# Finer pieces for the first weights, x and the third unit at the opening of a two-layer hybrid encoder trunk

## The reference

```python
for l in range(DEPTH):                      # DEPTH = 2
    h = rms_norm(x, ffn1_norm[l])
    x = x + 0.5 * swiglu(h, ffn1_w_gate[l], ffn1_w_up[l], ffn1_w_down[l])   # 1024 -> 2816 -> 1024
    h = rms_norm(x, mix_norm[l])
    p = h @ w_in[l]
    ...        # three groups of heads: forgetting attention, HGRN2 recurrence, S5 state space
    x = x + mix @ w_out[l]
    h = rms_norm(x, ffn2_norm[l])
    x = x + 0.5 * swiglu(h, ffn2_w_gate[l], ffn2_w_up[l], ffn2_w_down[l])
```

## Time and profile before

| what | value |
|---|---|
| median of 3 runs | 1035.27 us (1035.06 to 1035.53) |
| the profiled execution | 1035.68 us |
| its span, first to last instruction | 1033.7 us |
| PE busy | 1026.7 us, 99% of the span |
| DVE busy, ACT busy | 677.7 us (66%), 523.8 us (51%) |
| first matmul on zeros, first matmul of the FFN | 1.47 us, 8.69 us |

### The profile page before, as it was taken

How to read it: one execution, slowest core, us unless ns; L and a number is a source line. 1 busy time by engine, 2 the same in 40 slices (tenths; PEclk the granted TensorE clock), 3 DMA queues, 4 the chain that set the end, 5 groups by cost and what they waited for, 6 DMA issues and landing times.

```text
span 1033.7 us, 22792 instructions
## 1 busy us (share of the span) xinstructions
PE 1026.7 (99%) x9726; PEld 1010.9 (98%) x9726; DVE 677.7 (66%) x853; ACT 523.8 (51%) x630; POOL 202.8 (20%) x291
## 2 busy tenths in 40 slices
PE   8999999999999999999999999999999999999998
PEld 8999999999899999999999999999998999999998
DVE  7666656788668655555566666667987667555554
ACT  5645434565577534343475454436456765434331
POOL 0000899800002000000020019995000020000000
PEclk9999999999999999999999999999999999999999
DMA  8745454434325464645555555453432265454541
GB/s 299 268 157 208 165 199 161 161 133 156 125 83 204 163 210 161 204 160 202 178 203 206 180 186 203 162 204 123 161 128 88 88 235 201 166 203 162 203 162 42
DMA packets 26820, 178.40 MB, mean 173 GB/s; under 512 B 3120, under 2 KB 4160, under 8 KB 5760
## 3 DMA queue, kind: packets, MB, share of 16 engines
q1 hardware_dynamic: 25632, 173.03, 47.2%
q10 hardware_dynamic: 1008, 4.05, 1.1%
q0 software_dynamic: 112, 0.37, 0.1%
HBM read 176.38 MB, written 1.05 MB: 172 GB/s over the span
## 4 chain that ended last, share of the span: by engine, by line
PE 95%; DVE 2%; DMA 2%; ACT 1%; issue 0%; SPq 0%; DVEq 0%; ACTq 0%
PE ps L815 30%; PE ps L816 29%; PE ps L817 29%; DMA raw<-stream 2%; PE ps L968 1%; PE ps L1021 1%; PE ps L1086 1%; DVE in_lo L1422 0%; PE ps L1082 0%; PE ps L1043 0%; ACT hi L575 0%; PE ps L1062 0%; PE ps L1031 0%; PE ps L1149 0%; PE ps L1050 0%
## 5 line engine op out<-in xcount | busy, mean ns | idle before, releaser
L1221 DVE TENSOR_TENSOR lo<-raw,hi 128x2048 fp32r<-128x2048 f32 x130 | 300.7, 2322 | 202.2 <-ACT hi L575 202.2
L815 PE MATMUL ps<-xg_hi,hi 128*128 128x256 f32 x1408 | 399.3, 284 | 1.1 <-DVE lo L1305 0.7
L817 PE MATMUL ps<-xg_hi,lo 128*128 128x256 f32 x1408 | 398.4, 283 | 0.0
L816 PE MATMUL ps<-xg_lo,hi 128*128 128x256 f32 x1408 | 398.4, 283 | 0.0
L575 ACT ACTIVATE hi<-raw 128x2048 fp32r<-128x2048 f32 x130 | 247.1, 1909 | 175.7 <-PE ps L817 169.9
L815 PEld LDWEIGHTS ps<-xg_hi,hi 128*128 128x128 f32 x1408 | 270.3, 192 | 1.8 <-issue 1.7
L816 PEld LDWEIGHTS ps<-xg_lo,hi 128*128 128x128 f32 x1408 | 270.3, 192 | 0.1
L817 PEld LDWEIGHTS ps<-xg_hi,lo 128*128 128x128 f32 x1408 | 270.3, 192 | 0.0
L815 PE MATMUL ps<-act_hi,hi 128*128 128x256 f32 x704 | 199.4, 283 | 0.8 <-DVE act_lo L1259 0.8
L816 PE MATMUL ps<-act_lo,hi 128*128 128x256 f32 x704 | 199.2, 283 | 0.0
L817 PE MATMUL ps<-act_hi,lo 128*128 128x256 f32 x704 | 199.2, 283 | 0.0
(11 more groups left out here) (320 smaller groups left out, 1354.0 us busy)
## 6 DMA issues: line engine op xcount, KB each, us to landing
raw<-stream SPq DMA_DIRECT2D x160, 1024.0 KB, 4.9
par<-params ACTq DMA_DIRECT2D x2, 1463.0 KB, 9.0
raw<-stream SPq DMA_DIRECT2D x8, 256.0 KB, 7.4
rows<-stream SPq DMA_DIRECT2D x2, 1024.0 KB, 7.0
x<-xT ACTq DMA_DIRECT2D x4, 256.0 KB, 6.7
out<-x SPq DMA_DIRECT2D x8, 128.0 KB, 2.0
con<-consts POOLq DMA_DIRECT2D x1, 337.5 KB, 6.3
mask<-masks POOLq DMA_DIRECT2D x1, 20.0 KB, 6.5
```

Source lines behind the costliest of these rows:

```text
L815: pe.matmul(acc, w_hi, a_hi, start=start, stop=False, skip_group_check=True)
L816: pe.matmul(acc, w_hi, a_lo, start=False, stop=False, skip_group_check=True)
L817: return pe.matmul(acc, w_lo, a_hi, start=False, stop=stop, skip_group_check=True)
L1221: v.tensor_tensor(lo[slot][:, :], raw[slot][:, :], hi[slot][:, :].bitcast(F32), ALU.subtract).then_inc(lo_written, 1)
```

## The change

- **`FIRST`** replaces the four equal quarters of units 0 and 1 and of x by five pieces: tile 0, tile 1, then tiles 2 and 3, 4 and 5, 6 and 7. SP, ACT, DVE and PE all go by them, so ten weight pieces and five x pieces are loaded, and there are ten `hi` and ten `lo` operations. `x_loaded` and `first_loaded` have five semaphores each; GpSimd's constants still wait for tiles 2 and 3.
- **ACT's order of issue** is now x tile 0, the gains, x tile 1, the small copy with its table load, and then the three other pieces of x.
- **Unit 2** of the first FFN is loaded, split by ACT and split by DVE in four quarters. DVE's quarters stand behind the squares and ahead of `first_sums`, PE takes it by `third_unit`: input tile by input tile (k outside, m inside), as each quarter's low half is ready. `row_sums` moves into tile 7 of it.
- **PE's wait** at the start of the other FFN blocks is one wait for `lo_written` at tile 0, with the count that the parameter `begin` carried.
- **12 matmuls on zeros** instead of 18.

```diff
@@ -47,6 +47,7 @@
 QUARTERS = 4
+FIRST = [(0, 1), (1, 2), (2, 4), (4, 6), (6, 8)]
 IN_QUARTERS = QUARTERS * (IN_UNITS + OUT_UNITS)
@@ -251,8 +252,9 @@
         consts_loaded = sem("consts_loaded")
-        x_loaded = [sem(f"x_loaded{q}") for q in range(QUARTERS)]
-        first_loaded = [sem(f"first_loaded{q}") for q in range(QUARTERS)]
+        x_loaded = [sem(f"x_loaded{q}") for q in range(len(FIRST))]
+        first_loaded = [sem(f"first_loaded{q}") for q in range(len(FIRST))]
+        third_loaded = [sem(f"third_loaded{q}") for q in range(QUARTERS - 1)]
         first_hi = sem("first_hi")
@@ -355,15 +357,19 @@
         def _(sp):
-            for q in range(QUARTERS):
+            for q, (at, end) in enumerate(FIRST):
                 for s in range(2):
-                    c = slice(q * 512, (q + 1) * 512)
+                    c = slice(at * 256, end * 256)
                     sp.dma_start(raw[s][:, c], stream[s, :, c]).then_inc(first_loaded[q], 16)
...
 
+            for q in range(QUARTERS):
+                c = slice(q * 512, (q + 1) * 512)
+                sp.dma_start(raw[2][:, c], stream[2, :, c]).then_inc(third_loaded[q] if q < QUARTERS - 1 else raw_loaded[2], 16)
+
             def load_split(n, at, slot):
@@ -374,7 +380,8 @@
 
-                load_split(l * SPLIT_UNITS + 2, l * UNITS + 2, 2)
+                if l:
+                    load_split(l * SPLIT_UNITS + 2, l * UNITS + 2, 2)
                 with sp.Fori(1, ITERS) as i:
@@ -417,7 +424,7 @@
             pool.memset(lbs[:, 5, :], 0.0).then_inc(raw_loaded[1], 16)
-            pool.wait_ge(first_loaded[1], 32)
+            pool.wait_ge(first_loaded[2], 32)
             pool.dma_start(con[:, :], consts).then_inc(consts_loaded, 16)
@@ -613,22 +620,31 @@
 
-            e.dma_start(g0[:, :], gain0).then_inc(x_loaded[0], 16)
-            for q in range(QUARTERS):
-                e.dma_start(x[:, 2 * q:2 * q + 2, :], xT[:, 2 * q:2 * q + 2, :]).then_inc(x_loaded[q], 16)
-            e.wait_ge(once, 1)
-            e.activation(ln_ms[:, 0:1], eps[:, :], ACT.Copy)
-            for q in range(QUARTERS):
+            for q, (at, end) in enumerate(FIRST):
+                e.dma_start(x[:, at:end, :], xT[:, at:end, :]).then_inc(x_loaded[q], 16)
+                if q == 0:
+                    e.dma_start(g0[:, :], gain0).then_inc(x_loaded[0], 16)
+                if q == 1:
+                    e.wait_ge(once, 1)
+                    e.activation(ln_ms[:, 0:1], eps[:, :], ACT.Copy)
+            for q, (at, end) in enumerate(FIRST):
                 e.wait_ge(x_loaded[q], 32 if q == 0 else 16)
-                for m in (2 * q, 2 * q + 1):
+                for m in range(at, end):
                     e.activation(xg_hi[:, m, :], x[:, m, :], ACT.Copy, scale=g0[:, m:m + 1]
...
                 for s in range(2):
-                    c = slice(q * 512, (q + 1) * 512)
+                    c = slice(at * 256, end * 256)
                     e.activation(hi[s][:, c], raw[s][:, c], ACT.Copy
-                                 ).then_inc(first_hi if q < QUARTERS - 1 else hi_written, 1)
-            split_hi(2, 0, 2)
+                                 ).then_inc(first_hi if end < KT else hi_written, 1)
+            for q in range(QUARTERS):
+                c = slice(q * 512, (q + 1) * 512)
+                if q < QUARTERS - 1:
+                    e.wait_ge(third_loaded[q], 16)
+                else:
+                    e.wait_ge(raw_loaded[2], 16)
+                e.activation(hi[2][:, c], raw[2][:, c], ACT.Copy
+                             ).then_inc(first_hi if q < QUARTERS - 1 else hi_written, 1)
             e.wait_ge(consts_loaded, 32)
@@ -830,18 +846,17 @@
 
-            def ffn(f, n0, norm, begin):
+            def ffn(f, n0, norm):
                 head = f == 0
...
                     pe.wait_ge(xg_lo_ready, f * KT + k + 1)
-                    if k == 0:
-                        pe.wait_ge(lo_written, begin)
-                    if k == 6:
+                    starts = [at for at, end in FIRST]
+                    if k == (starts[-1] if head else 0):
                         pe.wait_ge(lo_written, n0 + 2 + RING)
-                    elif k % 2 == 0:
-                        pe.wait_ge(first_lo, k + 2)
+                    elif head and k in starts:
+                        pe.wait_ge(first_lo, 2 * starts.index(k) + 2)
                     if k == 5 and not head:
@@ -851,11 +866,9 @@
 
-                def gate_up(half, n, slot, b, between=lambda: None):
+                def gate_up(half, n, slot, b):
                     pe.wait_ge(lo_written, n + 1 + RING)
                     for m in range(2):
-                        if m == 1:
-                            between()
                         for k in range(KT):
@@ -863,11 +876,29 @@
 
+                def third_unit():
+
+                    for k in range(KT):
+                        if k == KT - 2:
+                            pe.wait_ge(lo_written, n0 + 3 + RING)
+                        elif k % 2 == 0:
+                            pe.wait_ge(first_lo, 2 * (len(FIRST) - 1) + k // 2 + 1)
+                        if k == KT - 1:
+                            row_sums(norm, False, 3)
+                        for m in range(2):
+                            w = k * 256 + m * P
+                            last = three(bank(6 + m)[:, 0:T], hi[2][:, w:w + P], lo[2][:, w:w + P],
+                                         xg_hi[:, k, :], xg_lo[:, k, :], k == 0, k == KT - 1)
+                    last.then_inc(units_done, 1)
+
                 def step(i, g, first=False):
...
                     pe.wait_ge(gu_read, f * ITERS + i + 1)
-                    gate_up(0, n, 2, 4 + 2 * g, lambda: row_sums(norm, False, 3) if head and first else None)
+                    if head and first:
+                        third_unit()
+                    else:
+                        gate_up(0, n, 2, 4 + 2 * g)
                     gate_up(1, n + 1, 0, 4 + 2 * g)
@@ -897,10 +928,10 @@
             pe.wait_ge(zeros_set, 1)
-            for _ in range(18):
+            for _ in range(12):
                 pe.matmul(bank(0), zero[:, 0:P], zero[:, :], start=True, stop=True, skip_group_check=True)
             for l in range(DEPTH):
-                ffn(l * 2, l * SPLIT_UNITS, l * 3, l * (SPLIT_UNITS + 2) + RING)
+                ffn(l * 2, l * SPLIT_UNITS, l * 3)
 
@@ -1208,7 +1239,7 @@
 
-                ffn(l * 2 + 1, l * SPLIT_UNITS + FFN_UNITS, l * 3 + 2, l * SPLIT_UNITS + FFN_UNITS + 2 + RING)
+                ffn(l * 2 + 1, l * SPLIT_UNITS + FFN_UNITS, l * 3 + 2)
 
@@ -1260,8 +1291,9 @@
             def ffn_steps(f, n0, norm, ahead, stages={}):
-                split_lo(n0 + 2, 2)
-                if f == 0:
+                if f:
+                    split_lo(n0 + 2, 2)
+                else:
                     first_sums()
@@ -1293,18 +1325,26 @@
             v.memset(forget_lo[:, :].bitcast(F32), 0.0).then_inc(rows_cleared, 1)
-            for q in range(QUARTERS):
-                for m in (2 * q, 2 * q + 1):
+            for q, (at, end) in enumerate(FIRST):
+                for m in range(at, end):
                     rest_of_x(0, m, g0)
                 for s in range(2):
-                    c = slice(q * 512, (q + 1) * 512)
-                    if q < QUARTERS - 1:
+                    c = slice(at * 256, end * 256)
+                    if end < KT:
                         v.wait_ge(first_hi, 2 * q + s + 1)
...
                     v.tensor_tensor(lo[s][:, c], raw[s][:, c], hi[s][:, c].bitcast(F32), ALU.subtract
-                                    ).then_inc(first_lo if q < QUARTERS - 1 else lo_written, 1)
+                                    ).then_inc(first_lo if end < KT else lo_written, 1)
             v.tensor_tensor(rows[:, :, :], x[:, :, :], x[:, :, :], ALU.mult).then_inc(first_squares, 1)
+            for q in range(QUARTERS):
+                c = slice(q * 512, (q + 1) * 512)
+                if q < QUARTERS - 1:
+                    v.wait_ge(first_hi, 2 * (len(FIRST) - 1) + q + 1)
+                else:
+                    v.wait_ge(hi_written, 3 + RING)
+                v.tensor_tensor(lo[2][:, c], raw[2][:, c], hi[2][:, c].bitcast(F32), ALU.subtract
+                                ).then_inc(first_lo if q < QUARTERS - 1 else lo_written, 1)
             v.wait_ge(consts_loaded, 32)
...
                 st = Steps(v, dve_step, l, DVE_STEPS)
```

## The result

| | median | range | runs |
|---|---|---|---|
| before, beside the change | 1035.43 us | 1035.06 to 1036.12 | 6 |
| the change | 1040.22 us | 1037.58 to 1041.33 | 6 |

The ratio is 1.0044, with an interval of 1.0034 to 1.0055. The change makes the kernel slower by 4.8 us; forecast were 1035.0 and no difference that can be measured. The five ordinary runs of the change took 1039.5 to 1041.3; the profiled one is the fastest of the six, 1037.58, so what it shows is the smaller part of the loss. A second profile, of an execution of 1040.47, stands with the experiments.

A forecast was written before the change was run, and what follows sets the result against it. PE was taken as the bound, behind an opening chain ending at 33.29 us; 0.2 of late packets less 0.5 of straggler put the down projection at 33.0, 0.3 earlier, hence 1035.0 us, range 1034.0 to 1036.1.

The forecast's parts named there:

- The frame: Opening: only PE's start and a second chain of loads, splits and activation, ending at 33.29 us, matter; behind it PE bounds.
- The first tile: Opening: with one tile to split instead of two, PE's first real matmul at about 7.45 us, a gain of 1.2.
- The step that held x's last transfers behind the table load: ACT's queue in the opening: x's tiles 2 to 7 are issued about 1.9 us later.
- the 0.3 us that this was to give the weights: Opening loads: with x issued later, weights sharing the DMA engines go ahead by part of it, taken as 0.3 us.
- The step that failed: Landing of weight tiles 2 and 3: small pieces cost 0.5 less 0.3 us, 0.2 late; PE stalls some 0.8 us.
- The term for the straggler: Load of unit 4: up to 1.1 us of its landing need not come again; half, 0.5 us, taken as gain.
- The clock: PE in the opening: twelve zero matmuls leave a 0.7 us gap; any slower matmuls are hidden in waits, cost nothing.
- the wait before the third unit: PE before the third unit: quarters remove this wait; the unit starts at 19.84 us, 1.05 earlier than at 20.89.
- C: Rival on opening loads: a 1 KB packet costs as much as a 2 KB one, 2.1 us; 1037.4 and slower; chance 0.06.
- E: Rival on PE's clock: it stays at 1.2 GHz through the first block, 10 us slower; chance 0.01.
- B: Rival on x's loads: x, landing 1.9 us later, becomes the head of the chain; 1035.5 to 1035.9; chance 0.17.
- D: Rival on the early start: PE starts at 8 or later, or 11.2 slips; chain stays; 1035.1 to 1035.5; chance 0.13.

The follow-up runs named there:

- the ordinary one: The changed kernel run once more unedited, for a profile of an ordinary execution: 1040.47 us, with the kernel before beside it at 1035.39.
- On one queue: Against the kernel with only weights and x in five pieces: SP issues the gains and x too, each x piece ahead of its weight pieces; 1038.20 us, ratio 1.0023.
- short rows: Kernel before, first four weight transfers still 256 KB but in 1 KB rows, split waiting for all four: 1040.24 us, ratio 1.0044.
- the run with fillers: The changed kernel plus 4 matmuls on zeros behind tile 0 and 13 behind tile 1 of the first block: 1039.27 us, ratio 1.0039.
- the two kernels with quick loads: Kernel before with unit 2 in quarters alone (1035.51 us, ratio 1.0002), and with that plus tiles 0 and 1 split singly on quarter loads (1035.76 us, ratio 1.0002).
- the control with long rows: Kernel before in old quarters with 2 KB rows, the weights' split starting only when the first four transfers have landed: 1037.75 us, ratio 1.0021.
- halves in the last quarter: Kernel before with the last quarter of units 0 and 1 loaded as two transfers each, of 64 partitions: 1036.81 us, ratio 1.0015.

## Why the prediction was wrong

**The frame held, with one gap.** The loss was made before the first down projection: from there to the end it is 1000.4 us before, 1000.2 in the profiled execution of the change and 1000.2 in the ordinary one. The links behind the load of unit 4 stayed as they were (9.64 us) in the profiled execution. In the ordinary one the two chains weren't as separate as the prediction has them: the second waited for PE at the split of unit 3. An early PE alone gains nothing: with tiles split singly it starts at 8.43 instead of the 8.71 of the run with the quarters of unit 2 alone, and waits 0.82 for the activation instead of 0.42; down starts at 32.87 and 32.82.

**The first tile** was forecast at 7.45 and ran at 6.25 (6.76 in the ordinary execution). The step that held x's last transfers behind the table load was wrong: they go out beside it. So was the 0.3 us that this was to give the weights.

**The step that failed** is "The third piece (tiles 2 and 3) is today's second quarter. Its second half landed at 2.14 + 6.9 = 9.04", with 384 packets at 22 ns, 0.5 less 0.3 us, as all that the small pieces cost. They landed at 11.84 in the profiled execution and at 12.9 in the ordinary one, 2.8 to 3.9 us later. In place of a stall of 0.8 at 10.3 PE had waits of 1.10 and 3.35. The runs with one part alone, with weights or x alone, and with the small pieces last show that four small weight transfers at the head of the queue do most of it (1.0023 of the 1.0039 of all pieces), and x's small ones beside them the rest.

The step priced packets alone and took the order of service as it was. Two things were missing. One is the rate: from 7 to 9 us 160 to 270 GB/s with the engines at a share of 0.75 to 0.93, in every kernel with small weight transfers ahead, and 290 or more in all others of 128 partitions. By the estimate above that is about 1.2 of the 2.8 us. The other is the order, about 1.5: bytes of later pieces and of x were moved before those of tiles 2 and 3. In the ordinary execution, where 3.02 MB had been moved at the landing, the same estimate gives 1.4 and 2.4, in the run with the weights alone in pieces 0.4 and 1.7. On one queue the order kept and the dip stayed. Why the engines have gaps while issued transfers wait, and why the piece is overtaken, stays open; no run shows the engines singly. The long eighth issue isn't needed for the dip, which comes without it in two runs.

**The term for the straggler** was wrong too: half of 1.1 us was to go, and the load of unit 4 took 7.72, 7.74 and 7.74 where it took 7.78. It took 6.65 in the ordinary execution of the change and 6.67 with short rows, but there PE was what the chain waited for. What makes the difference is open.

**The clock** was put at nothing, with a stall of 0.8 us as cover. That holds for the twelve matmuls alone. Behind a real wait of 4.24 us it did not: 2.6 us of slower matmuls went into the opening, and through the split of unit 3 into the second chain as well. The Trainium skill's "TensorE: Matmul & The Clock Gate", section "HAM oscillation — how this bites in real kernels", says that waits for transfers between groups of matmuls drop the engine to half its clock; the ordinary execution agrees (4.24 us, then 0.50), while the profiled one waited 3.35 us and kept its full clock. The clock's share of the 4.8 us is an estimate: 1.5 us if the down projection at 38.29 is set against the 36.81 of the run with fillers, whose tiles 2 and 3 landed 0.2 us later still, and 2.6 at most. The ratio of the run with fillers doesn't separate it.

**What went right**: the wait before the third unit goes (down at 32.82 and 32.87 in the two kernels with quick loads, forecast 33.0), and the quarters cost nothing. That the 33.0 was nearly met is luck: the straggler that was to bring it stayed, and unit 4 was issued 0.4 us sooner, which no term had. **The rivals**: C, small pieces slow, had the sign and 1037.4, from 2.1 us on; the chain's shift was 2.2 in the profiled execution, which took 1037.58. It had a chance of 0.06. The clock behind its wait was in no rival but the full one, E. B fell, since x is not held back, D as well. The rule of the Trainium skill cited with C, that small transfers reach a fraction of the rate of 1 MB, points the way the runs do; its 138 GB/s is lower than any stretch from 7 to 9 us here (162 and more), and its estimate of 1038 lies between the two profiled executions.

## What to carry to other kernels

Splitting the first load to start sooner pays only if the piece that follows still lands in time, and small transfers at the head of a queue need a price of their own where no row of the trace has one (here 0.5 to 0.8 us for each small transfer of weights, by the ratios of the runs with two and with four). The price isn't only in their own bytes: a piece queued behind them on one of two queues can be overtaken by later ones, so the landing to forecast is that of the piece that is wanted next. Where a second chain caps an early start, its gain is bounded and its risk is not; splitting the work on data that are loaded as before has the same start without that risk. A wait of a few us on the matrix engine is priced with the slower clock that may follow it, not by its length alone.

## What the runs showed of the hardware

- ACT issues transfers while it loads a function table: three issues from 2.23 to 3.59 beside a load from 2.17 to 3.45.
- Halving a row from 2 to 1 KB at the same size of transfer made the fourth transfer land 1.9 us later, with only 0.1 MB less moved by 9 us; the rest of the delay is in what was served first.
- Transfers issued on one queue can land out of order: in the change the one issued at 3.57 us landed at 11.3, the one issued at 3.10 at 11.84 (in the ordinary execution 11.6 and 12.9).
- PE stood idle for up to 0.96 us with no releaser in the profile near 243 to 248 us in 13 of 20 profiles, and not in the others.
- Transfers of 64 partitions were slow in both places tried: 243 GB/s from 7 to 9 us at the head, and 245 at a share of 1.13 in the last quarter, where their ratio was 1.0015.
- After the wait of 4.24 us in the change PE ran at the lower clock for 5.7 us, busy all the time. With the pieces alone, where the wait was 3.88, the matmul behind it took 0.35 us as at full clock, and the granted clock fell later, to 0.64 from 15 to 17 us and 0.51 from 17 to 19, with PE at work since 14.36. In the control with long rows a wait of 2.54 had the lower clock behind it (first matmul 0.55, granted clock 0.50 from 11 to 13), in the profiled execution of the change one of 3.35 had not. With halves in the last quarter even a wait of 2.26 us, behind 6 us of work without a break, had the lower clock behind it (first matmul 0.55). The length of the wait alone doesn't tell.
